# One kernel, three rearrangements: order of the decay gates' products, an earlier slice of each head's query product, earlier copies of weights at the norms

## The reference

```
h  = _modulate(_rms(x, norm_attn), mod_x[0], mod_x[1])        # 512 tokens
hc = _modulate(_rms(ctx, norm_attn), mod_c[0], mod_c[1])      # 256 context tokens
beta = sigmoid(beta_logit)                                    # of h @ w and of hc @ w
g = -exp(a_log) * softplus(decay_logit + dt_bias)
q, k, v = split(silu(_centred_conv(h @ w_qkv, conv_w)))       # then q, k scaled to unit length per head
for each head, chunk by chunk, in both directions:            # gc: cumulative sum of g
    v_new = u_i - w_i @ s;  o_i = qd_i @ s + qk_i @ v_new;  s = s * gl_i + kd_i.T @ v_new
```

## Time and profile before

| | us |
|---|---|
| median of 3 runs | 4576.3 |
| lowest and highest | 4576.24, 4578.54 |
| the profiled execution | 4592.87 |
| its span | 4591.1 |
| mean granted clock in it | 0.946 |

### The profile page before, as it was taken

How to read it: one execution, slowest core, us unless ns; L and a number is a source line. 1 busy time by engine, 2 the same in 40 slices (tenths; PEclk the granted TensorE clock), 3 DMA queues, 4 the chain that set the end, 5 groups by cost and what they waited for, 6 DMA issues and landing times.

```text
span 4591.1 us, 47689 instructions
## 1 busy us (share of the span) xinstructions
PE 4229.6 (92%) x19046; PEld 3123.7 (68%) x19046; DVE 2042.7 (44%) x3049; ACT 1220.7 (27%) x1699; POOL 1441.9 (31%) x834
## 2 busy tenths in 40 slices
PE   7999999899999699989998997879898899998999
PEld 5656788556788378866557885556666665684887
DVE  6567323264413541355763332356665346503322
ACT  3322222134222122233232221223232124421222
POOL 3311344100444144433013442175656000241343
PEclk9999999999999799999999998889999889999999
DMA  6200222210232123222002221211121121222232
GB/s 175 74 21 21 103 103 83 101 46 28 97 111 87 55 93 114 87 74 73 10 28 101 95 100 53 68 33 55 31 57 26 68 83 56 74 92 69 83 97 83
DMA packets 96909, 333.72 MB, mean 73 GB/s; under 512 B 44336, under 2 KB 47536, under 8 KB 67888
## 3 DMA queue, kind: packets, MB, share of 16 engines
q1 hardware_dynamic: 87968, 311.85, 19.9%
q10 hardware_dynamic: 8720, 18.82, 1.6%
HBM read 317.53 MB, written 13.11 MB: 72 GB/s over the span
## 4 chain that ended last, share of the span: by engine, by line
PE 78%; DVE 14%; POOL 3%; ACT 2%; issue 2%; DMA 1%; SPq 0%; DVEq 0%; ACTq 0%; POOLq 0%
PE bank L878 16%; PE bank L879 16%; PE bank L880 15%; PE bank L1301 5%; PE bank L858 4%; PE bank L1080 2%; PE bank L867 2%; PE bank L1030 2%; PE bank L1054 2%; PE bank L1597 1%; DVE xn L2288 1%; PE bank L1596 1%; PE bank L1618 1%; PE bank L1528 1%; PE bank L1410 1%
## 5 line engine op out<-in xcount | busy, mean ns | idle before, releaser
L773 POOL TENSOR_TENSOR w_lo<-ring,w_hi 128x2048 fp32r<-128x2048 f32 (+2 forms) x200 | 774.8, 3874 | 1575.2 <-ACT w_hi L1733 1575.2
L878 PE MATMUL bank<-x_hi,w_hi 128*128 128x512 f32 x1584 | 619.5, 391 | 16.4 <-POOL w_lo L773 16.4
L879 PE MATMUL bank<-x_lo,w_hi 128*128 128x512 f32 x1584 | 617.9, 390 | 0.0
L880 PE MATMUL bank<-x_hi,w_lo 128*128 128x512 f32 x1584 | 617.8, 390 | 0.0
L1733 ACT ACTIVATE w_hi<-ring 128x2048 fp32r<-128x2048 f32 (+2 forms) x200 | 322.0, 1610 | 877.7 <-PE bank L880 876.8
L878 PE MATMUL bank<-h_hi,w_hi 128*128 128x512 f32 x960 | 374.1, 390 | 0.3
L880 PE MATMUL bank<-h_hi,w_lo 128*128 128x512 f32 x960 | 373.7, 389 | 0.0
L879 PE MATMUL bank<-h_lo,w_hi 128*128 128x512 f32 x960 | 373.6, 389 | 0.0
L878 PEld LDWEIGHTS bank<-x_hi,w_hi 128*128 128x128 f32 x1584 | 298.2, 188 | 81.2 <-POOL w_lo L773 19.7
L880 PEld LDWEIGHTS bank<-x_hi,w_lo 128*128 128x128 f32 x1584 | 298.3, 188 | 62.2
L879 PEld LDWEIGHTS bank<-x_lo,w_hi 128*128 128x128 f32 x1584 | 298.2, 188 | 61.4
(11 more groups left out here) (448 smaller groups left out, 7437.3 us busy)
## 6 DMA issues: line engine op xcount, KB each, us to landing
ring<-stream SPq DMA_DIRECT2D x212, 1024.0 KB, 4.8
ring<-stream SPq DMA_DIRECT2D x64, 704.0 KB, 4.0
ring<-stream SPq DMA_DIRECT2D x36, 512.0 KB, 3.6
xn<-first_mods SPq DMA_DIRECT2D x8, 1024.0 KB, 5.8
ring<-stream SPq DMA_DIRECT2D x4, 1088.0 KB, 5.1
bias_rows<-work ACTq DMA_DIRECT2D x1, 4096.0 KB, 46.1
work<-bias_rows ACTq DMA_DIRECT2D x1, 3072.0 KB, 11.7
tab<-tabs ACTq DMA_DIRECT2D x1, 2624.0 KB, 16.4
```

Source lines behind the costliest of these rows:

```text
L773: nc.gpsimd.tensor_tensor(w_lo[:, j % 2, 0:cols], ring[:, k % RING, 0:cols], w_hi[:, j % 2, 0:cols], ALU.subtract).then_inc(wlo_set, 1)
L878: mm(b[:], hi[:, at + k, :], rhs_hi, start=(k == 0), stop=False)
L879: mm(b[:], hi[:, at + k, :], rhs_lo[:, k, :], start=False, stop=False)
L880: ins = mm(b[:], lo[:, at + k, :], rhs_hi, start=False, stop=(k == kt - 1))
```

## The change

Five edits.

1. In `decays` TensorE takes the sequence chunks (2 to 5) first and waits for the context only ahead of chunk 0. After these products, and ahead of the wait for the gates, it does head 0's whole query product. `proj` skips it later.
2. In `gdn` the first half of the query product of head t+1 moves from the start of iteration t+1 to iteration t, ahead of `rows`, for t = 0 to 7.
3. At a norm ahead of a feed-forward part ScalarE copies weight block 0 after the fifth square, and block 1 after the sixth. For the layer behind the pooling mixer block 0 stays after the eighth square and block 1 in `ffn`. For the last MLP only block 0 moves (to after the fifth square).
4. At the norm ahead of the second Hyena the copy of its first weight block moves from after the root to after the fifth square.
5. The high part of the last Hyena output block goes to another buffer.

```diff
-        out_hi = [..., hyena_parts["hyena_hi"][:], hyena_parts["out_hi"][:, 0]]
+        out_hi = [..., hyena_parts["hyena_hi"][:], halves_of[2][0]]
...
+            first_w = []
             def decays(_):
                 pe.wait_ge(xn_set, n["xn"])
-                pe.wait_ge(ctx_set, 1)
...
-                for c in range(CH):
+                for c in list(range(2, CH)) + [0, 1]:
+                    if c == 0:
+                        pe.wait_ge(ctx_set, 1)
                     for k in range(DT):
                         ins = mm(b[:, 32 * c:32 * (c + 1)], tokens(c)[:, k, :], w[:, k, :], ...)
                 ins.then_inc(aux_full, 1)
+                for t in range(acc.n - BANKS, acc.n):
+                    drained(acc, acc_drained, t)
+                first_w.append(weights())
+                for k in range(DT):
+                    ins = mm(banks[P_BANKS[0]][:], first_w[0][:, k, :], xn[:, k, :], ...)
+                ins.then_inc(p_full, 1)
                 pe.wait_ge(gate_set, 2)
...
                 def proj(name, h, lo, hi):
+                    if name == "q" and h == 0:
+                        return
...
-                    proj("q", new, 0, 4)
+                    if not 0 < t <= GH:
+                        proj("q", new, 0, 4)
...
                     if new < GH:
+                        proj("q", new + 1, 0, 4)
                         rows("nq", new, t, 0, 4)
...
+            def after_pool(then):
+                return then[0] == "ffn" and then[1] % 3 == 2
+            def two_early(then):
+                return then[0] == "ffn" and not after_pool(then)
             def norm(gain, then=None):
...
                     signal(go(xn[:, k, :], x[:, k, :], ACT.Square), squares_set)
-                if then:
-                    split(*then, 0)
+                    if then and k == (DT - 1 if after_pool(then) else 4):
+                        split(*then, 0)
+                    if then and k == 5 and two_early(then):
+                        split(*then, 1)
+                    if k == 4 and first >= 0 and split_target(gain) == "hyena":
+                        high_weights(starts[("hyena", gain[1] // DT // 3)], in_hi[0])
                 t = full(aux, aux_full)
                 signal(go(rstd, ..., ACT.Sqrt, bias=eps_col, scale=1.0 / D), root_set)
                 if split_target(gain) == "hyena":
-                    high_weights(starts[("hyena", gain[1] // DT // 3)], in_hi[0])
+                    if first < 0:
+                        high_weights(starts[("hyena", gain[1] // DT // 3)], in_hi[0])
                     split_x(x_hi_h)
...
             def ffn(layer):
-                        split("ffn", layer, j + 1)
+                        if j or not two_early(("ffn", layer)):
+                            split("ffn", layer, j + 1)
```

More of the change, by code:

```diff
@@ L336, in build_program @@
         in_hi = halves_of[0] * 4 + [halves_of[1][0], halves_of[1][1], halves_of[1][0], hyena_parts["hyena_hi"][:]]
-        out_hi = [hyena_parts["out_hi"][:, 0], hyena_parts["out_hi"][:, 1], hyena_parts["hyena_hi"][:], hyena_parts["out_hi"][:, 0]]
+        out_hi = [hyena_parts["out_hi"][:, 0], hyena_parts["out_hi"][:, 1], hyena_parts["hyena_hi"][:], halves_of[2][0]]
         IN_BLOCK = list(range(11)) + [13]
@@ L1209, in decays @@
                 ins.then_inc(aux_full, 1)
+                for t in range(acc.n - BANKS, acc.n):
+                    drained(acc, acc_drained, t)
+                first_w.append(weights())
+                for k in range(DT):
+                    ins = mm(banks[P_BANKS[0]][:], first_w[0][:, k, :], xn[:, k, :], start=(k == 0), stop=(k == DT - 1))
+                ins.then_inc(p_full, 1)
                 pe.wait_ge(gate_set, 2)
@@ L1246, in gdn @@
                 until = TB2("until").rearrange("p (d i) -> p d i", d=2)
-                head_w, opened = {}, {}
+                head_w, opened = {(0, 0): first_w[0]}, {}
                 def a_tile(*name):
@@ L1745, in high_weights @@
                 signal(go(high, ring[:, k % RING, 0:2 * DT * P], ACT.Copy), whi_set)
+            def after_pool(then):
+                return then[0] == "ffn" and then[1] % 3 == 2
+            def two_early(then):
+                return then[0] == "ffn" and not after_pool(then)
             def norm(gain, then=None):
                 first = acc.n - DT
+                if gain is not None and gain[0] == "norm_ffn":
+                    then = ("ffn", gain[1] // DT)
                 for k in range(DT):
@@ L1754, in norm @@
                     signal(go(xn[:, k, :], x[:, k, :], ACT.Square), squares_set)
-                if gain is not None and gain[0] == "norm_ffn":
-                    then = ("ffn", gain[1] // DT)
-                if then:
-                    split(*then, 0)
+                    if then and k == (DT - 1 if after_pool(then) else 4):
[4 more added lines that the diff above has]
+                        high_weights(starts[("hyena", gain[1] // DT // 3)], in_hi[0])
                 t = full(aux, aux_full)
```

## The result

| | before | changed |
|---|---|---|
| median, us | 4577.4 (4 runs) | 4529.9 (4 runs) |
| lowest and highest | 4576.24, 4580.02 | 4525.42, 4534.13 |
| the profiled execution | 4592.87 | 4525.42 |
| its span, mean granted clock | 4591.1, 0.946 | 4523.6, 0.955 |

The kernel before has one run more here than in the table ahead of the prediction. The ratio is 0.9895, 95% interval [0.9878, 0.9912]: 47.5 us less, where 42.6 were forecast (4534; range 4527 to 4549). A second measurement, beside other runs of the kernel before, gave 0.991 [0.989, 0.993].

The account below looks back on a forecast made before the run. TensorE, busy 92% of the span, was taken as the bound, so only its idle or half-clock time could be won. Gains of 19.2 + 13.2 + 10.2 = 42.6 us off the 4576.3 us median gave 4534, range 4527 to 4549.

Parts of the forecast that it names:

- Term 1: Decays: sequence products before the context's win 9.8 us, head 0's query product in the gates' wait 9.4; 19.2 us.
- just fits: Decays: head 0's query product, starting at half clock, takes 9.4 us and fits TensorE's 9.46 us wait for the gates.
- rival 3: After the decays: late z or head blocks, or the solve chain, take up the head start; 4553 us, chance 0.04.
- Term 2: Delta net boundaries: four query products put ahead of the previous iteration's rows win 13.2 us, bounds about 0 to 17.7.
- (a): Delta net boundaries: the early query products fill the wait ahead of the rows, 3.85 us first, 3.06 to 3.42 later.
- (b): Delta net boundaries: ten row products run at full clock, 2.4 us instead of 3.97 to 4.4, winning 1.5 us.
- (c): Fourth chunk product: with its cover gone TensorE waits 2.1 us for a bank and gets 1.3 of the 3.44 us.
- Term 3: Early weight copies: three feed-forward waits go, 7.4 us, and the second Hyena's norm wins 2.8; 10.2 us, bounds 7 and 11.
- The smallest sum: Whole kernel: the lower bounds 16.7 + 5 + 7 give a gain of 28.7 us, the slow end at 4548 us.
- Rival 4: Delta net boundaries: half clock through slice, rows and products behind costs 11.3 us each, seven cost 79; 4626 us, chance 0.03.

Follow-up runs that it names:

- edit 1 alone: The kernel before with only the decays' sequence tokens first and head 0's query product in the wait for the gates: 4559.2 us, ratio 0.9955.
- edit 2 alone: The kernel before with only four products of the next head's query moved ahead of the rows: 4562.8 us, ratio 0.9968.

## Why the prediction was right, and where its terms were off

**Term 1 (19.2 us; measured 18.4 in its stretch, 20.6 by the ratio).** The order of the tokens: 9.8 forecast, 10.2 measured. The query product: 9.4 forecast, 9.4 to 10.0 measured from the small products to z. With edit 1 alone z starts 19.6 us sooner behind the norm, and the missing 1.1 us lie behind z, where kernels without the slice differ by as much. The step that it "just fits" the wait of 9.46 us depended on the clock: the product took 9.9 us in the profile of the changed kernel, since the clock came back later, and overran by 0.4; with edit 1 alone it took 8.9 and left 0.73. z's weights were there in time, and no data movement took anything back (rival 3).

**Term 2 (13.2 us; measured 12.4 in its stretches, 14.6 by the ratio).** The stretch with the first two boundaries gave 2.0 where 2.7 were forecast for the first and nothing for the second. How much of it is the slice is open: from z to iteration 2 it takes 121.7 to 122.9 us in the four kernels without the slice, 120.9 with edit 2 alone, and 120.5 and 122.5 in the two profiles of the changed kernel. The wait for solved blocks, 12.96 us before, was 13.3 with edit 2 alone and 14.7 and 17.1 in those two: it takes up what is won in iteration 1. The six others: 10.5 forecast, 10.4 and 11.6 measured (edit 2 alone, and all edits). That this sum is so near is partly luck. Parts (a) and (b) were right; (c), the bank wait, was right in size (1.97 for 2.1) but left out what the clock does behind it, 1.2 to 1.7 us more at five boundaries. Against that stood a gain not counted either: I let three of the six boundaries lose 2.7 us in a slice at half clock, where it takes 3.6 to 4.4 us in the changed kernel and not 5.9. An iteration takes 74.5 to 75.5 us there, where before it took 76.0 to 77.8.

**Term 3 (10.2 us; measured 13.3).** This is the mis-sized term. The 2.8 us at the second Hyena came as worked out, and so did the cause: with the subtraction over instructions that have one input in PSUM nothing is held, with it over those with two in SBUF the pair waits. The Trainium skill (SBUF — State Buffer, section Who interferes with whom) has this rule, and the traces agree in both directions, 4.36 us and 1.54. The three feed-forward waits were put at their rows, 1.55 + 2.76 + 3.09 = 7.4 us, and are worth 3.2 + 3.0 + about 4.2 = 10.4: a wait that depends on the half clock at the stage's start, and a second fall of the clock behind it.

**The range.** The smallest sum takes 5 us for term 2 (16.7 + 5 + 7), while the part on the slice gives about 0 as that term's own bound. No row shows the 5; with 0 the range would have ended near 4553. Nothing hung on it, since the measured time lies 3 us from the other end.

**The difference of the profiles.** I took the 42.6 us over to the median and not to the profiled execution, whose 16.6 us above the median I left in place. That held: they are Hyena steps at half clock, and the profiles' 67.5 us would have been the wrong thing to explain with the edits.

**Rival 4 (slower).** It let the clock stay at half through slice and rows. Where the slice started at half clock it got the full one back within itself (5.4 us at the longest, at the end of iteration 1), and the rows behind it were at full clock at all eight boundaries.

## What to carry to other kernels

Price a wait of TensorE with what the clock does behind it: rows of 1.6 to 3.5 us were worth 3.0 to 5.4 here, and a wait that a change brings can cost more than its row too. When a slice of dense work is moved into one wait, look at the place it leaves; here two more products in the new gap were worth another 18 us in the stretch and 22 by the ratios. Compare profiles stretch by stretch between rare instructions before explaining their total, since untouched stretches differed by 20 us.

## What the runs showed of the hardware that I had not expected

- The clock fell from 1.00 to 0.50 while TensorE was busy without a gap, inside 32 one-column sums, which took 4.67 us in place of 3.63; the 8 dense products behind took 9.4 in place of 7.1 us. In other executions of the same instructions it didn't. In 18 groups cut in two with dense products between, it never did.
- After a wait of 2.0 us in the delta net TensorE's next four products took 4.8 to 5.3 us in place of 3.6 at five boundaries and 3.6 at three; after one of 1.37 the rows ran at full clock, after one of 3.55 they didn't.
- After a wait of 3.09 us the clock fell some 0.9 us behind it, with the engine busy again, and came back 3.4 us later. The length of the wait doesn't decide it alone: behind 2.76 us (layer 1 before) the clock held, and behind 1.79 us (layer 2 with edit 2 alone, where no edit works) it fell.
- The half clock at the start of a feed-forward stage lasted from 2.8 to 6.2 us in the same code.
